# Attention stages with the first two units of a head pair joined: two stretches a pair instead of three

## The reference, cut to what matters

```python
# mixer_a, per block of 128 queries: keys chosen by an index score, a distance bias
logits = einsum('bqhd,bqkhd->bhqk', qb, ks) * DH_A ** -0.5 + bias
logits = where(valid[:, None], logits, NEG)
out    = einsum('bhqk,bqkhd->bqhd', softmax(logits), vs)        # then out @ w_out
# mixer_b, per block of 128 queries: chunk-causal, heads of 96 for the scores, 64 for the values
logits = einsum('bqhd,bshd->bhqs', qb, k) * scale
logits = where((pos[None, :] < lim[:, None])[None, None], logits, NEG)
out    = einsum('bhqs,bshd->bqhd', softmax(logits), v)          # then out @ w_out
```

## Time and profile before

| | |
|---|---|
| Profiled execution: its own time | 1252.3 us |
| its span, first to last instruction | 1250.4 us |
| Median of the three timed runs | 1251.67 us |
| PE busy | 1215.3 us, 97% of the span |
| DVE / ACT / POOL busy | 763.2 / 545.9 / 216.5 us |
| Share of PE in the chain that ended last | see the rows below |
| Attention 0 on PE | about 194 to 269.5 us |
| Attention 1 on PE | about 764.5 to 843.9 us |

### The profile page before, as it was taken

One profiled execution on the slowest core, in us unless ns is written; L12 is line 12 of the kernel. 1 busy time (PEld: TensorE's weight loads), 2 busy tenths in 40 slices (PEclk: granted clock), 3 DMA queues, 4 the chain that ended last, 5 costly groups with the idle time before them and its releaser, 6 DMA issues.

```text
span 1250.4 us, 17161 instructions
## 1 busy us (share of the span) xinstructions
PE 1215.3 (97%) x6052; PEld 971.6 (78%) x6052; DVE 763.2 (61%) x1315; ACT 545.9 (44%) x931; POOL 216.5 (17%) x262
## 2 busy tenths in 40 slices
PE   7999999999999999999999878999999999999998
PEld 5758876678788888878888766778788888887887
DVE  4588976646766565663337778763775656664334
ACT  5554345645534343333226676643543433343222
POOL 4423433411200000000004663430400000000000
PEclk9999999999999999999999999999999999999999
DMA  6522222212322222212233100012322222212323
GB/s 234 192 93 87 83 78 60 69 51 101 108 101 94 101 101 101 84 61 91 101 101 105 50 20 1 1 35 101 130 73 101 101 101 101 90 62 84 101 92 110
DMA packets 25120, 110.83 MB, mean 89 GB/s; under 512 B 2752, under 2 KB 3136, under 8 KB 17776
## 3 DMA queue, kind: packets, MB, share of 16 engines
q1 hardware_dynamic: 25072, 110.21, 25.5%
HBM read 108.06 MB, written 6.33 MB: 91 GB/s over the span
## 4 chain that ended last, share of the span: by engine, by line
PE 88%; DVE 6%; POOL 2%; issue 2%; ACT 2%; DMA 1%; SPq 0%; DVEq 0%; POOLq 0%; ACTq 0%
PE ps L1737 25%; PE ps L1739 24%; PE ps L1738 24%; PE ps L1498 3%; PE ps L1517 3%; PE ps L1388 2%; PE ps L1376 2%; DVE h_lo L954 1%; DVE xT L1151 1%; DVE w_lo L948 1%; PE ps L1371 1%; PE ps L1482 1%; PE ps L1410 1%; PE ps L1709 1%; POOL rope_tmp L490 1%
## 5 line engine op out<-in xcount | busy, mean ns | idle before, releaser
L948 DVE TENSOR_TENSOR w_lo<-raw,w_hi 128x1024 fp32r<-128x1024 f32 (+4 forms) x114 | 195.2, 1712 | 260.9 <-ACT w_hi L582 260.9
L1737 PE MATMUL ps<-h_hi,w_hi 128*128 128x512 f32 (+1 forms) x712 | 278.6, 391 | 2.5 <-DVE w_lo L948 2.5
L582 ACT ACTIVATE w_hi<-raw 128x1024 fp32r<-128x1024 f32 (+4 forms) x124 | 177.8, 1434 | 230.3 <-PE ps L1739 230.3
L1738 PE MATMUL ps<-h_lo,w_hi 128*128 128x512 f32 (+1 forms) x712 | 277.8, 390 | 0.0
L1739 PE MATMUL ps<-h_hi,w_lo 128*128 128x512 f32 (+1 forms) x712 | 277.8, 390 | 0.0
L1737 PE MATMUL ps<-a_hi,w_hi 128*128 128x512 f32 x480 | 188.0, 392 | 2.1 <-DVE w_lo L948 1.6
L1738 PE MATMUL ps<-a_lo,w_hi 128*128 128x512 f32 x480 | 186.8, 389 | 0.0
L1739 PE MATMUL ps<-a_hi,w_lo 128*128 128x512 f32 x480 | 186.8, 389 | 0.0
L1737 PEld LDWEIGHTS ps<-h_hi,w_hi 128*128 128x128 f32 (+1 forms) x712 | 133.6, 188 | 32.1 <-DVE w_lo L948 3.4
L1738 PEld LDWEIGHTS ps<-h_lo,w_hi 128*128 128x128 f32 (+1 forms) x712 | 133.7, 188 | 28.3 <-issue 0.6
L1739 PEld LDWEIGHTS ps<-h_hi,w_lo 128*128 128x128 f32 (+1 forms) x712 | 133.5, 188 | 28.4 <-issue 0.7
(11 more groups left out here) (188 smaller groups left out, 1510.7 us busy)
## 6 DMA issues: line engine op xcount, KB each, us to landing
raw<-in_f_up SPq DMA_DIRECT2D x44, 1024.0 KB, 4.8
raw<-in_f_w_down SPq DMA_DIRECT2D x44, 512.0 KB, 3.3
raw<-in_a_in_wide SPq DMA_DIRECT2D x13, 1024.0 KB, 4.8
bias_tiles<-bias_rows SPq DMA_DIRECT2D x1, 4096.0 KB, 19.7
raw<-in_a_w_out SPq DMA_DIRECT2D x8, 512.0 KB, 3.2
raw<-in_b_w_out SPq DMA_DIRECT2D x8, 512.0 KB, 3.3
xT<-in_xt SPq DMA_DIRECT2D x4, 512.0 KB, 6.5
toep_b<-bias_tiles SPq DMA_DIRECT2D x8, 256.0 KB, 3.2
```

What stands on the lines that cost most here:

```text
L582: sc.activation(w_hi[:, s, 0:n], raw[:, s, 0:n], ACT.Copy).then_inc(w_hi_done, 1)
L948: dve.tensor_tensor(w_lo[:, s, 0:n], raw[:, s, 0:n], w_hi[:, s, 0:n].bitcast(F32), ALU.subtract)\
L1737: pe.matmul(dst, s_hi, m_hi, start=start, stop=False)
L1738: pe.matmul(dst, s_hi, m_lo, start=False, stop=False)
```

## The change

The two `attention(n)` lists are rewritten on PE, ACT and DVE. A pair now has two stretches. In the first, PE does turn(u), turn(u+1), scores(u+3), scores(u+4), mix(u-1); in the second turn(u+2), scores(u+5), mix(u), mix(u+1), with u = 3i. `probsT` gets a third buffer (in attention 0 a part of `act` that is free by then, in attention 1 space over the bias tiles) and is taken by u % 3. The number of instructions and their shapes stay the same. For the last pair, `early_rows` 0 stands in the place of scores(u+3) and scores(u+4), `early_rows` 1 in that of scores(u+5). POOL's list is unchanged.

```diff
--- before.py
+++ after.py
@@ -244,12 +244,15 @@
             kv_lo = sb("kv_lo", [P, D], F32R, scope)
         probs0, probs1 = sb("probs0", [P, 2, S]), sb("probs1", [P, 2, S])
         probs3 = sb("probs3", [P, 2, S])
+        with ExitStack() as scope:
+            third_b = sb("third_b", [P, 2, S], F32, scope)
         toep_b1 = sb("toep_b1", [P, S])
         sb("pad_h0", [P, S])
         probs2 = sb("probs2", [P, 2, S])
         toep_a1, toep_b0 = sb("toep_a1", [P, S]), sb("toep_b0", [P, S])
         probs = [probs0, probs1, probs2, probs3]
-        probsT = [sb(f"probsT{j}", [P, 2, S]) for j in range(2)]
+        turned0, turned1 = sb("probsT0", [P, 2, S]), sb("probsT1", [P, 2, S])
+        probsT = [[turned0, turned1, act[:, 16:18]], [turned0, turned1, third_b]]
         toep = [[rope_tmp[:].rearrange("p a n -> p (a n)"), toep_a1], [toep_b0, toep_b1]]
 
 
@@ -729,7 +732,7 @@
 
                 sc.wait_ge(t_ok[n], 2 * u + e + 1)
                 w = U_COLS[u % 3]
-                sc.activation(probsT[u % 2][:, e, 0:w], ps[:, turn_bank(u, e), 0:w], ACT.Copy)\
+                sc.activation(probsT[n][u % 3][:, e, 0:w], ps[:, turn_bank(u, e), 0:w], ACT.Copy)\
                     .then_inc(pt_act[n], 1)
 
             def pair_out(n, i):
@@ -744,20 +747,27 @@
                 sc.activation(a_hi[:, b, :], act[:, kk, :], ACT.Copy).then_inc(r_hi[n], 1)
 
             def attention(n):
-                for s in range(UNITS):
-                    if s >= 4 and s % 3 == 1:
-                        pair_out(n, s // 3 - 1)
-                    if s == UNITS - 4:
+                exps(n, 2, 0)
+                exps(n, 2, 1)
+                for i in range(PAIRS):
+                    u = 3 * i
+                    if i + 1 < PAIRS:
+                        exps(n, u + 3, 0)
+                        exps(n, u + 3, 1)
+                    else:
                         act_hi(2 * n, 0, 0, True)
-                    if s + 2 < UNITS:
-                        exps(n, s + 2, 0)
-                    if s == UNITS - 2:
+                    if i:
+                        pair_out(n, i - 1)
+                    if i + 1 < PAIRS:
+                        exps(n, u + 4, 0)
+                        exps(n, u + 4, 1)
+                    else:
                         hi((U_AOUT, U_BOUT)[n] + 1)
                         act_hi(2 * n, 1, 1, True)
-                    if out_by_scalar(s, 1):
-                        turned_probs(n, s, 1)
-                    if s + 2 < UNITS:
-                        exps(n, s + 2, 1)
+                    turned_probs(n, u + 2, 1)
+                    if i + 1 < PAIRS:
+                        exps(n, u + 5, 0)
+                        exps(n, u + 5, 1)
                 pair_out(n, PAIRS - 1)
 
             def onto_residual(n, u0, tiles, n_next, gain_at, nxt):
@@ -1111,7 +1121,7 @@
 
                 dve.wait_ge(t_ok[n], 2 * u + e + 1)
                 w = U_COLS[u % 3]
-                dve.tensor_copy(probsT[u % 2][:, e, 0:w], ps[:, turn_bank(u, e), 0:w]).then_inc(pt_dve[n], 1)
+                dve.tensor_copy(probsT[n][u % 3][:, e, 0:w], ps[:, turn_bank(u, e), 0:w]).then_inc(pt_dve[n], 1)
 
             def act_lo(n, kk, b):
                 dve.wait_ge(r_hi[n], kk + 1)
@@ -1119,21 +1129,27 @@
                     .then_inc(r_lo[n], 1)
 
             def attention(n):
-                for s in range(UNITS):
-                    if s + 1 < UNITS:
-                        inverse_sums(n, s + 1)
-                    if s == UNITS - 3:
+                inverse_sums(n, 1)
+                for i in range(PAIRS):
+                    u = 3 * i
+                    for j in range(2):
+                        for e in range(2):
+                            turned_probs(n, u + j, e)
+                    inverse_sums(n, u + 2)
+                    if i + 1 < PAIRS:
+                        logits(n, u + 3)
+                        logits(n, u + 4)
+                        inverse_sums(n, u + 3)
+                    else:
                         act_lo(2 * n, 0, 0)
-                    for e in range(2):
-                        if not out_by_scalar(s, e):
-                            turned_probs(n, s, e)
-                    if s + 3 < UNITS:
-                        logits(n, s + 3)
-                    if n == 1 and s == UNITS - 4:
+                    turned_probs(n, u + 2, 0)
+                    if i + 1 < PAIRS:
+                        logits(n, u + 5)
+                        inverse_sums(n, u + 4)
+                    if n == 1 and i == PAIRS - 2:
                         lo(U_BOUT)
-                    if s == UNITS - 2:
-                        lo((U_AOUT, U_BOUT)[n] + 1)
-                        act_lo(2 * n, 1, 1)
+                lo((U_AOUT, U_BOUT)[n] + 1)
+                act_lo(2 * n, 1, 1)
 
             def onto_residual(n, u0, tiles, n_next, gain_at, nxt):
                 with dve.Fori(0, tiles // 2 - 1) as i:
@@ -1515,7 +1531,7 @@
                     for e in range(2):
                         h = 2 * i + e
                         ins = pe.matmul(ps[e * DH:(e + 1) * DH, 7, b * P:(b + 1) * P],
-                                        v[:, kb, h * DH:(h + 1) * DH], probsT[u % 2][:, e, c * P:(c + 1) * P],
+                                        v[:, kb, h * DH:(h + 1) * DH], probsT[n][u % 3][:, e, c * P:(c + 1) * P],
                                         start=kb == 0, stop=kb == b)
                 if j == 2:
                     ins.then_inc(o_ok[n], 1)
@@ -1535,16 +1551,24 @@
                     tile_product(d, b, b == 0, False)
 
             def attention(n):
-                for s in range(UNITS):
-                    turn(n, s)
-                    if s + 3 < UNITS:
-                        scores(n, s + 3)
-                    if s:
-                        mix(n, s - 1)
-                    if s == UNITS - 2:
+                for i in range(PAIRS):
+                    u = 3 * i
+                    turn(n, u)
+                    turn(n, u + 1)
+                    if i + 1 < PAIRS:
+                        scores(n, u + 3)
+                        scores(n, u + 4)
+                    else:
                         early_rows(2 * n, 0)
-                    if s == UNITS - 1:
+                    if i:
+                        mix(n, u - 1)
+                    turn(n, u + 2)
+                    if i + 1 < PAIRS:
+                        scores(n, u + 5)
+                    else:
                         early_rows(2 * n, 1)
+                    mix(n, u)
+                    mix(n, u + 1)
                 mix(n, UNITS - 1)
 
             def onto_residual(n, u0, tiles):
```

## The result

The changed kernel takes 1263.64 us (median of four runs, 1262.95 to 1264.62) against 1251.6 us (four runs, 1250.31 to 1251.99) on the same chip: ratio 1.0098, 95% interval 1.0082 to 1.0114. It is slower by about 1%; 1262.9 us was predicted. The profiled execution of after took 1263.01 us with a span of 1261.1 us, 10.7 us more than the 1250.4 us of before.

The account below looks back on a forecast made before the run. PE's own issue, plus whatever makes it wait, was taken to bound the kernel. First attention +5.8, second +3.3 and clock +2.1 gave +11.2 us on the profiled 1252.3, 1263.5; the median, 0.6 lower, 1262.9 us; range 1257.5 to 1267.

Parts of the forecast that it names:

- The switches: PE changing between kinds of work: joining stretches saves 0.17 us a pair in the first attention, 0.30 in the second.
- The unknown entry: First attention, scores now followed by mask products: cost of entering the mask, bounds 0 and 0.10 us, taken as 0.03.
- The bank: Four halves turned in a row with three banks: PE waits for a copy, 0.24 us a pair in both attentions.
- POOL: Turn of unit u+4 waits for POOL: 0.49 us a pair in the first attention; in time in the second.
- First pairs: First pair of each attention: +0.1 us in the first (bank only), +0.3 in the second (POOL work no longer hidden).
- The ends: Last pair: stalls of 1.5 us before early_rows 0 and 2.8 before early_rows 1; +3.8 us first attention, +3.4 second.
- the meeting of lo and POOL: End of the second attention: POOL waits out DVE's lo of the first weight tile, a stall of 0.6 us.
- The clock: Granted clock falls to half behind the pause before early_rows 1: 2.1 us for both attentions together.
- The sum: Whole kernel: +5.8 us first attention, +3.3 second, +2.1 clock, +11.2 us in all; median 1262.9 us.
- Rival 1: Ends of the attentions: stalls hidden, only the steady part counts, +1.9 us, 1253.6 us; chance 0.05.
- Rival 2: Bank copy and POOL's unit u+4 come in time, only the switches remain: 3.3 us less, 1248.4 us; chance 0.05.
- Rival 3: Steady pairs drift, POOL falling behind another 0.5 us a pair in both attentions: + 7 us, 1269.9 us; chance 0.08.

Follow-up runs that it names:

- e4: Changed kernel with DVE's copy of half (u, 0) of units j = 0 cut from 384 to 128 columns, result incomplete, PE work full size: 1263.92 us.
- e6: Kernel of e5 with half (u+1, 1) turned later: behind the next mask products in attention 0, behind the first half of the scores in attention 1; 1247.62 us.
- e3: Changed kernel with DVE's inverse_sums(u+4) put ahead of logits(u+5): 1259.38 us.
- e1: Changed kernel with act_hi and act_lo of pair 0 put one pair earlier on ACT and DVE: 1261.25 us.
- e2: Changed kernel, last pair re-ordered: early_rows 0 behind mix(20), early_rows 1 behind mix(22), DVE's lo and act_lo of step 1 ahead of the last copy: 1253.24 us.
- e5: Changed kernel with the edits of e1, e2 and e3 together: 1250.64 us.

## Why the prediction was right

**The switches.** Predicted 0.30 us saved a pair in the second attention: 9.59 - 9.29 (e4, where neither bank nor POOL waits) = 0.30. Predicted 0.17 in the first, with the mask products behind the scores as its unknown: 9.11 - 8.92 = 0.19 (e6). The unknown entry, bounded by 0 and 0.10, came out near 0, and after's own timeline shows it: 8 score products followed by the mask take 224.37 - 223.52 = 0.85 us, as the same 8 products followed by a turn took in before (196.17 - 195.32), and the mask products behind them 224.80 - 224.37 = 0.43, for 0.42 behind a turn. The Trainium skill, "TensorEngine Tiling (Array Packing)", section "Key Properties", on which the higher bound would have rested, says that a change of tiling mode drains TensorE. It is not contradicted: the drain may lie in the exit that stayed, but nothing here shows one beyond it.

**The bank.** Predicted 0.24, measured 0.21 (e3 and e6 in the first attention, e4 and e6 in the second). **POOL.** Predicted 0.49 with the bank hidden in it (its own figures give 5.49 + 0.33 - 3.98 - 1.37 = 0.47); 0.50 from after's own starts, and 9.43 - 9.13 = 0.30 when only POOL's part goes (e3). The pairs so came out at 9.42 and 9.50 for 9.43 and 9.53.

**First pairs.** +0.32 us in the second attention for +0.3. In the first -0.11 for +0.1: the bank wait is there (e4 removed 0.22), so the rest of the pair got 0.33 shorter, more than the 0.17 of a steady pair, which I had not worked out; the sign was missed, but the term is small.

**The ends.** Predicted stalls 1.5 and 2.8 us, of which 1.3 and 2.6 would be visible as pauses; PE's pauses are 1.40 and 2.57 us, with DVE's a_lo as releaser. First end 16.33 for 16.2. In the second the meeting of lo and POOL makes 837.82 - 836.57 = 1.25 us of six transposes that need 0.71, a stall of 0.54 for the 0.6 put down; but another 0.25 follow at 838.34, where the bank wait, which I had taken as covered, shows once more. early_rows 0 begins 840.29 - 836.57 = 3.72 us into that end, for 1.37 + 0.6 + 1.5 = 3.47, and without the clock's 1.55 the end is 16.6 us for 16.3. e1 takes away the first pause alone; e2 takes away the second and all but 0.38 us of the first, and by re-ordering alone returns the ends to 12.66 and 12.95.

**The clock.** The one term that was mis-sized by more than 0.3 us: 2.1 us predicted, 1.55 measured in this execution, as one fall in two ends. The two ends have the same pause between the same instructions, and e2, which has no such pause, has no fall in its ends. Timeline of PE behind it in the second end, where the fall comes at 849.4:

```profile
847.92 0.47 PE L1761 MATMUL ps<-a_hi,w_hi 128*128 128x512 f32 x1 [2.57 <-DVE a_lo L1128]
...
849.38 0.60 PE L1761 MATMUL ps<-a_hi,w_hi 128*128 128x512 f32 x1
849.78 0.63 PE L1762 MATMUL ps<-a_lo,w_hi 128*128 128x512 f32 x1
```

Products start every 0.42 us in place of 0.23. From the first product to the end of the attention it is 854.73 - 847.92 = 6.81 us, in the first end 275.25 - 269.99 = 5.26: 1.55 more. Over the profiled executions of after, e1, e3 and e4 five of eight such pauses have a fall, with prices of 1.4 to 1.6 us. That makes 1.9 us on average for the two ends. The four runs of after spread over 1.7 us, about the price of one fall, but their mean clocks (0.993 to 0.996) don't put their times in order, so that the spread is not shown to be the clock's. The prediction looked at one pause of before; two more falls in that trace, behind pauses of 1.95 us (to 679.13, with products right before and behind it) and 1.75 us (to 755.38), it left unused. What decides whether a given pause has a fall stays open.

**The sum.** As measured it is 5.7 + 5.0 = 10.7 us for the 11.2 predicted: 5.7 for 5.8 in the first attention, 3.5 for 3.3 in the second without its fall, 1.55 for 2.1 of the clock. The mechanism held term by term. That the median came within 0.7 us is in part luck. The medians rose by 12.0 us, the profiled executions by 10.7, and the 1.3 us between these are in no trace; the forecast put the median 0.6 us below the profiled execution, and in after it lies 0.6 above. The clock's term, 0.55 too high, made up for part of that.

None of the three rivals came true. Rival 1 (the end stalls hidden) put after at 1253.6 us, which is where e2, with the end stalls nearly gone, stands (1253.24). Rival 2 (the switches alone) put it at 1248.4 us, near e6 (1247.62), though e6's ends are shorter too. Rival 3's drift isn't there: six pairs in a row are equal to 0.01 us.

## What to carry to other kernels

Joining stretches saves only entries and exits (0.2 to 0.3 us a pair here), and moves some consumers nearer to their producers. Before joining, count the buffers in rotation (three banks, four halves in a row) and look at what each in-order engine has queued ahead of the value that is awaited. Look at the last iteration by itself: what the code puts in the place of the missing work may depend on something that was only just started. Two such places an attention made 9.2 of the 10.7 us (1.55 of it by the fall of the clock behind one of them). A short wait can be filled by moving the piece that waits behind a little of the next work (e6), where the switch between the operations costs nothing.

## What the runs showed of the hardware

**A fall of the clock can be free.** Between the attentions all nine kernels of this case have the same pause of about 2.65 us. The clock fell there in five (before, e1, e2, e3, e6) and not in the other four. The PE timeline, waits alone, of before and of after:

```profile
738.90 1.97 PE L1709 MATMUL ps<-con,tok 128*96 128x128 f32 x16 [0.92 <-DVE tok L1289]
```

```profile
737.72 1.95 PE L1733 MATMUL ps<-con,tok 128*96 128x128 f32 x16 [2.64 <-DVE tok L1305]
...
744.69 1.95 PE L1733 MATMUL ps<-con,tok 128*96 128x128 f32 x16 [2.27 <-DVE tok L1305]
```

From the one wait to the next it is 738.90 - 731.97 = 6.93 us with the fall and 744.69 - 737.72 = 6.97 without: the slower products only ate into the next pause, 0.92 us instead of 2.27. In all nine kernels this stretch takes 6.93 to 6.97 us. In the ends of the attentions no further wait follows, and there a fall costs its 1.4 to 1.6 us.

**A fall elsewhere moves the time of a whole kernel.** Behind a pause of 1.95 us near 680 us, which all nine kernels have too, the clock fell in before, after, e2, e4 and e5. From the product behind that pause to the end of the next pause it is 17.93 to 17.97 us in these five (after: 702.87 - 684.91 = 17.96) and 16.46 to 16.48 us in the other four (e3: 701.33 - 684.87 = 16.46): 1.5 us that no edit of this case has touched. In e4 and e5 a later fall, behind the pause of 1.75 us, lasts about twice as long as in the others and costs another 1.0 us. So the stretch between the attentions takes 493.7 to 496.2 us in the nine profiled executions, and an edit worth less than that is read from its own stretch, not from the time.

**Switches.** Between 128-row transposes, the bf16 mask products and 96-row scores none was measurable (transposes start at their usual 0.11 us); going into a mix and out of it costs the 0.15 us of the prediction: the 24 products of e6 take 789.08 - 787.62 = 1.46 us, 24 x 0.055 = 1.32 and 0.14.
